# Gated layers: the norm's row factor put onto the gate and up outputs, their inputs split tile by tile, squares added on GpSimd

## What is computed

```
def rmsnorm(x, gain):
    y = xf * lax.rsqrt(jnp.mean(xf * xf, axis=-1, keepdims=True) + EPS)
    return y * gain
def swiglu(h, w_gate_up, w_down):
    gate, up = jnp.split(h @ w_gate_up, 2, axis=-1)
    return (jax.nn.silu(gate) * up) @ w_down
for i in range(DEPTH_2):                       # 2 layers
    h = rmsnorm(x, norm_mix[i])
    x = x + (s5_mixer(h, ...) if i == 0 else dsa_mixer(h, ...))
    x = x + swiglu(rmsnorm(x, norm_ffn[i]), ffn_w_gate_up[i], ffn_w_down[i])
```

## Time and profile before

| what | value |
|---|---|
| time, median of 3 runs | 3164.7 us (3161.42 to 3247.57) |
| the profiled execution | 3160.65 us, span 3158.8 us, clock 0.96 |
| PE busy | 2900.4 us, 92% of the span |
| DVE busy | 1864.0 us, 59% |
| ACT busy | 1393.9 us, 44% |
| POOL busy | 219.7 us, 7% |
| L348 by high_b and weight_parts | 1872 matmuls, 398 ns mean each |
| L716 low part of weights | 185, 1226 ns mean |
| L708 high part of weights | 185, 1060 ns mean |

### The profile page before, as it was taken

The page is one execution under the profiler, slowest core; times in us unless marked ns, Lnnn a source line. Parts: engine busy times, 40 slices in busy tenths (PEclk is TensorE's granted clock), DMA queues, the critical chain, the costliest instruction groups (busy, mean ns, idle before and its releaser), DMA issues.

```text
span 3158.8 us, 35772 instructions
## 1 busy us (share of the span) xinstructions
PE 2900.4 (92%) x12800; PEld 2235.7 (71%) x12800; DVE 1864.0 (59%) x2206; ACT 1393.9 (44%) x1794; POOL 219.7 (7%) x167
## 2 busy tenths in 40 slices
PE   7999999985899999999993678999989999989998
PEld 2548878765677777777772566788867767768887
DVE  3435653564988888888887753333236685343322
ACT  2323233223667777777775323323223435333221
POOL 1100100003930000000001000000001100000000
PEclk9999999996999999999997879999999999999999
DMA  6921722314899989999993802222221110122221
GB/s 236 330 76 60 282 85 94 121 62 161 319 331 352 387 351 387 361 377 369 369 372 108 107 32 75 94 95 106 93 75 67 67 54 1 41 72 101 94 94 67
DMA packets 90801, 546.92 MB, mean 173 GB/s; under 512 B 9232, under 2 KB 18848, under 8 KB 32384
## 3 DMA queue, kind: packets, MB, share of 16 engines
q1 hardware_dynamic: 79584, 485.65, 41.6%
q0 software_dynamic: 10816, 59.58, 5.5%
q10 hardware_dynamic: 288, 0.15, 0.0%
HBM read 516.51 MB, written 41.42 MB: 177 GB/s over the span
## 4 chain that ended last, share of the span: by engine, by line
PE 69%; DVE 17%; issue 6%; DMA 4%; ACT 3%; SPq 1%; POOL 1%; DVEq 0%; ACTq 0%; PEldq 0%; POOLq 0%
PE bank L348 38%; PE bank L286 6%; PE bank L1138 5%; PE bank L1142 4%; PE bank L1141 4%; DVE expert_low L2218 4%; DMA arena<-in_we_stream 2%; ACT expert_high L1587 1%; PE bank L1370 1%; PE bank L1392 1%; PE bank L1383 1%; DMA arena<-in_mod 1%; PE bank L1122 1%; DVE expert_x_low L2303 1%; DVE arena L2320 1%
## 5 line engine op out<-in xcount | busy, mean ns | idle before, releaser
L2218 DVE TENSOR_TENSOR expert_low<-arena,expert_high 128x2048 fp32r<-128x2048 f32 x291 | 684.2, 2382 | 102.7 <-ACT expert_high L1587 85.4
L1587 ACT ACTIVATE expert_high<-arena 128x1024 fp32r<-128x1024 f32 x582 | 597.2, 1057 | 213.4 <-PE bank L1138 117.5
L348 PE MATMUL bank<-high_b,weight_parts 128*128 128x512 f32 x1872 | 592.9, 398 | 29.6 <-DVE low_b L2456 15.9
L716 DVE TENSOR_TENSOR weight_parts<-ring_pages,weight_parts 128x1024 fp32r<-128x1024 f32 x185 | 226.7, 1226 | 557.9 <-ACT weight_parts L708 557.4
L708 ACT ACTIVATE weight_parts<-ring_pages 128x1024 fp32r<-128x1024 f32 x185 | 196.1, 1060 | 591.6 <-PE bank L348 552.4
L348 PEld LDWEIGHTS bank<-high_b,weight_parts 128*128 128x128 f32 x1872 | 352.8, 190 | 121.1 <-issue 36.3
L348 PE MATMUL bank<-low_b,weight_parts 128*128 128x512 f32 x832 | 325.7, 391 | 0.0
L1138 PE MATMUL bank<-expert_high,expert_x_low 128*128 128x512 f32 x768 | 309.5, 403 | 14.1 <-DVE expert_low L2218 10.4
L1141 PE MATMUL bank<-expert_high,expert_x_high 128*128 128x512 f32 x768 | 301.1, 392 | 0.0
L1142 PE MATMUL bank<-expert_low,expert_x_high 128*128 128x512 f32 x768 | 300.6, 391 | 0.0
L348 PE MATMUL bank<-hidden_parts,weight_parts 128*128 128x512 f32 x1056 | 240.0, 389 | 4.3 <-DVE hidden_parts L2502 4.3
(11 more groups left out here) (464 smaller groups left out, 4033.2 us busy)
## 6 DMA issues: line engine op xcount, KB each, us to landing
arena<-in_we_stream SPq DMA_DIRECT2D x294, 1024.0 KB, 6.5
ring_pages<-in_wb_stream SPq DMA_DIRECT2D x93, 1024.0 KB, 4.8
ring_pages<-in_wa_stream SPq DMA_DIRECT2D x49, 1024.0 KB, 4.9
arena<-in_mod POOLq DMA_DIRECT2D x16, 1024.0 KB
xbuf<-arena POOLq DMA_DIRECT2D x25, 512.0 KB, 15.9
arena<-xbuf SPq DMA_DIRECT2D x17, 512.0 KB, 7.3
ybuf<-arena SPq DMA_DIRECT2D x16, 512.0 KB, 2.6
arena<-kd SPq DMA_DIRECT2D x8, 512.0 KB, 24.1
```

What stands on the lines that cost most here:

```text
L348: ins = pe.matmul(o, lhsT, rhs, start=start, stop=stop)
L716: nc.vector.tensor_tensor(low, src, high.bitcast(F32), ALU.subtract).then_inc(weights_split, 1)
L1587: nc.scalar.activation(ehigh[c % HIGH_E][:, at], ring_e[c % RING_E][:, at], ACT.Copy) \
L2218: nc.vector.tensor_tensor(elow[c % RING_E][:], ring_e[c % RING_E], ehigh[c % HIGH_E][:].bitcast(F32), ALU.subtract).then_inc(weights_split ...
```

## The change

The norm of a gated layer commutes with its products: (x * gain * RS) @ W is ((x * gain) @ W) * RS, since RS is one number per token. The change uses that.

- The gated layers' input is now x * gain only. `ffn_tile` (ScalarE) makes its high part straight from `x` with the gain as the scale, and then the tile's square; `ffn_low` (VectorE) makes the low part from `x`, gain and high part in one instruction. Both stand in the loops of the product ahead (`glu`, `wo`), one tile behind the tile of `x` that was just finished.
- `sn2` and `sn4` stand behind the first gate block (`gu00`, `gu10`). Their root and reciprocal are taken after the weight splits of the first pair.
- For each gate block VectorE first writes gate * RS into `st` (an added instruction), ScalarE applies silu in place, VectorE writes up * RS into `product` (was the product with silu) and multiplies by `st` there (added).
- GpSimd adds the eight squares into the first (`squares_summed`, seven additions), and TensorE multiplies only the sum by ones. This holds for `sn3` too. For `sn3` the squares stay behind the last `down` block's splits, and `normed_all` stays.
- `low_g`, `hid_late`, `ffn_in` and the new place of the third squares move buffers, so that inputs of a gated layer can be written while the product ahead still reads its own.

```diff
-JOBS_B += [f"glu{b}" for b in range(2 * KT)] + ["sn2"]
-JOBS_B += [f"gu0{b}" for b in range(2 * FFT)] + [f"down0{j}" for j in range(KT)] + ["sn3"]
+JOBS_B += [f"glu{b}" for b in range(2 * KT)] + ["gu00", "sn2"]
+JOBS_B += [f"gu0{b}" for b in range(1, 2 * FFT)] + [f"down0{j}" for j in range(KT)] + ["sn3"]
...
+            def squares_summed(n):
+                for kt in range(1, KT):
+                    pool.wait_ge(S["b_sq_full"], KT * (n - 2) + kt + 1)
+                    link(nc.gpsimd.tensor_tensor(sqb[n][:, 0, :], sqb[n][:, 0, :], sqb[n][:, kt, :], ALU.add))
+                pool.sem_inc(S["sq_summed"], 1)
+
+            squares_summed(2)
+            squares_summed(3)
             pool.wait_ge(S["b_x_ready"], 2 * KT)
...
             def squares(n):
                 ps = opened(f"sn{n}")
-                for kt in range(KT):
-                    pe.wait_ge(S["b_sq_full"], KT * (n - 2) + kt + 1)
-                    ins = pe.matmul(ps[:], ones[:], sqb[n][:, kt, :], start=(kt == 0), stop=(kt == KT - 1))
-                ins.then_inc(bank_done, 1)
+                pe.wait_ge(S["sq_summed"], n + 1)
+                pe.matmul(ps[:], ones[:], sqb[n][:, 0, :], start=True, stop=True).then_inc(bank_done, 1)
...
+            def ffn_tile(n, kt):
+                act.wait_ge(S["b_x_ready"], KT * 2 * n + kt + 1)
+                nc.scalar.activation(ffn_in[n][0][:, kt, :], x[:, kt, :], ACT.Copy, scale=col("norm_ffn", KT * n + kt)) \
+                    .then_inc(high_ready, 1)
+                squared_tile(2 + 2 * n, kt)
...
             def dense_act(n, n_sig):
-                high_part(high_b, raw, S["b_h_full"], h_count[2 + 2 * n] - KT)
                 for j in range(FFT):
                     weights_high_part(act, ahead(f"down{n}", f"gu{n}", 2 * j), split_to)
-                    ps = result(act, f"gu{n}{2 * j}")
-                    act.wait_ge(S["b_st_used"], n_sig - 1)
+                    if j == 0:
+                        rooted(2 + 2 * n)
                     n_sig += 1
-                    copied(act, nc.scalar.activation(st[:, j % 2, :], ps[:], ACT.Silu), S["b_sig_b"], n_sig,
-                           f"gu{n}{2 * j}")
+                    act.wait_ge(S["b_st_given"], n_sig)
+                    nc.scalar.activation(st[:, j % 2, :], st[:, j % 2, :], ACT.Silu).then_inc(S["b_sig_b"], 1)
...
+            def ffn_low(n, kt):
+                n_high[0] += 1
+                dve.wait_ge(high_ready, n_high[0])
+                high, low = ffn_in[n]
+                nc.vector.scalar_tensor_tensor(out=low[:, kt, :], in0=x[:, kt, :], scalar=col("norm_ffn", KT * n + kt),
+                                               in1=high[:, kt, :].bitcast(F32), op0=ALU.mult, op1=ALU.subtract) \
+                    .then_inc(split_ready, 1)
...
             def dense_dve(n, n_sig, n_x):
-                normed_all(2 + 2 * n, "norm_ffn", KT * n, low_b)
                 for j in range(FFT):
...
+                    gate, up = f"gu{n}{2 * j}", f"gu{n}{2 * j + 1}"
+                    weights_low_part(dve, ahead(f"down{n}", gate[:3], 2 * j), split_to)
+                    if j == 0:
+                        rms(2 + 2 * n)
                     n_sig += 1
+                    copied(dve, nc.vector.tensor_tensor(st[:, j % 2, :], result(dve, gate)[:], RS[:], ALU.mult),
+                           S["b_st_given"], n_sig, gate)
+                    if j < FFT - 1:
+                        weights_low_part(dve, ahead(f"down{n}", gate[:3], 2 * j + 1), split_to)
+                    link(nc.vector.tensor_tensor(product[:, j % 3, :], result(dve, up)[:], RS[:], ALU.mult))
+                    dve.sem_inc(free(up), 1)
                     dve.wait_ge(S["b_sig_b"], n_sig)
...
+                    nc.vector.tensor_tensor(product[:, j % 3, :], product[:, j % 3, :], st[:, j % 2, :], ALU.mult) \
+                        .then_inc(product_ready, 1)
```

74 lines of the change are left out of this document (44 added, 30 removed).

## The result

| what | before | after |
|---|---|---|
| median of the timed runs | 3243.11 us (3161.42 to 3256.53, 20 runs) | 3139.07 us (3132.32 to 3228.15, 20 runs) |
| the profiled execution | 3160.65 us | 3138.67 us |
| ratio of compared runs | | 0.9946, 95% interval 0.9924 to 0.9969 |

Launches of either kernel fall into levels. Over all series of this study, the kernel before has 40 of its 71 launches at 3156 to 3166 us and 31 at 3238 to 3257; the changed kernel has 20 of 33 at 3128 to 3141, 12 at 3157 to 3175 and one at 3228. The ratio leaves out every run more than 1.5% above the lowest of its series: here the highest level alone, in experiments 1, 7 and 9 also one or two runs of the middle one, so the ratios of different series can't be set side by side. The two medians are 104 us apart only because 12 of the 20 launches before are of the highest level.

What follows compares the result with a forecast made beforehand. TensorE's products bound it, broken only where a norm stands between two; 17.7 + 17.7 - 0.4 - 1.7 - 1.8 = 31.5 us off 3160.65 gives 3129.2, plus 1: 3130 us, range 3124 to 3140.

Steps and rivals of the forecast that it cites:

- Start of layer 0: From the end of glu: gu00 follows at once, gu01 starts 17.7 us earlier with contention, 19.5 without.
- Rival (b): GpSimd's additions do not disturb VectorE at layer 0 and sn3 loses only 0.9 us: 3127 us, chance 0.12.
- Start of layer 1: From the end of wo: no contention expected, gu11 starts 17.7 us earlier.
- gu03's weights: Their split stands behind root, reciprocal and silu; just fits, 0.2 us lost per layer, 1.3 if the table load shows.
- Rival (c): The row factor's chain is longer than summed, gu03 comes 1 to 4 us late per layer: 3136 us, chance 0.13.
- Inside the layers: Two more VectorE instructions of 0.69 us per pair of blocks fit into free time and cost nothing.
- rival (e): The longer chain per pair makes each weight split late: slower, 3200 us at 5 us more per pair, chance 0.02.
- rival (d): gu00 or gu10 still waits for the norm, so one layer's start stays as it is: 3148 us, chance 0.04.
- Ends of the layers: Ahead of the down blocks the gap grows from 2.17 to 3.0 us: 0.85 lost, twice, 1.7 us.
- Rival (a): The clock falls behind the new 3.0 us gaps at both gated layers' ends, about 3 us each: 3136 us, chance 0.22.
- sn3: The norm behind layer 0's down blocks waits for seven additions: 1.8 us lost, bounds 0.9 and 1.8, cossin fetch hidden.
- The sum: All terms over the launch: 17.7 + 17.7 - 0.4 - 1.7 - 1.8 = 31.5 us gained, forecast 3130 us.

Runs made afterwards that it cites:

- experiment 1: The changed kernel again, no edit, beside the kernel before: median 3138.34 us against 3165.67, ratio 0.9961.
- experiment 7: Changed kernel with third-norm squares made one by one beside the down blocks and the row factor on the gate alone: median 3148.15 us, ratio 0.9881 to the kernel before.
- experiment 9: The kernel of experiment 7 again, no further edit: median 3154.35 us, ratio 0.9946.
- experiment 3: Changed kernel without the GpSimd additions, TensorE multiplying all eight squares again: 3135.99 us, one execution.
- Experiment 2: Kernel before with only the GpSimd additions of squares, TensorE multiplying the sum: 3259.94 us, one execution.
- experiment 4: Changed kernel with only sn3's squares back on TensorE, without additions there: 3135.17 us, one execution.
- experiment 5: Changed kernel with sn3's squares made one by one beside the down blocks, additions kept: 3213.28 us, one execution.
- experiment 6: Changed kernel with the row factor on the gate's silu alone, one instruction fewer behind the last up block: 3205.98 us, one execution.
- 10 to 12: Thirteen more matmuls in the attention's loop, in the kernel before, the changed one and that of experiment 7: medians 3183.42, 3146.15 and 3138.19 us.

## Why the prediction was right or wrong

**Start of layer 0: right, 1.0 us too little.** gu00 follows `glu` at once and gu01 starts 7.17 us later. I had 8.1. The order of contention was as told, addition 6, low part 6, addition 7, low part 7:

```profile
1965.07 1.29 POOL L920 TENSOR_TENSOR arena<-arena 128x512 f32<-128x512 f32 x1 [8.42 <-ACT arena L1669]
1966.78 1.29 POOL L920 TENSOR_TENSOR arena<-arena 128x512 f32<-128x512 f32 x1 [0.41 <-ACT arena L1669]
```
```profile
1965.44 1.47 DVE L2496 SCALAR_TENSOR_TENSOR low_b<-arena,cols,high_b 128x512 fp32r<-128x512 f32 x1 [0.24 <-DVE arena L2509]
...
1966.84 1.78 DVE L2496 SCALAR_TENSOR_TENSOR low_b<-arena,cols,high_b 128x512 fp32r<-128x512 f32 x1
```

Each low part ends 0.55 us behind its addition (1966.91 behind 1966.36, 1968.62 behind 1968.07), where I had 0.8, and the four overlap a little more than I let them, so TensorE lost 1.3 us and not 1.9. Rival (b), that the additions do not disturb VectorE, falls with experiment 3.

The matmul of the sum was right at 0.88, but only half of it lies ahead of gu01. gu01's first two matmuls are followed by the next after 0.88 us, where in the steady stream it is 0.46:

```profile
1969.94 1.03 PE L348 MATMUL bank<-high_b,weight_parts 128*128 128x512 f32 x2
1970.82 0.40 PE L348 MATMUL bank<-low_b,weight_parts 128*128 128x512 f32 x1
1971.05 0.62 PE L348 MATMUL bank<-high_b,weight_parts 128*128 128x512 f32 x2
1971.51 0.40 PE L348 MATMUL bank<-low_b,weight_parts 128*128 128x512 f32 x1
...
1981.27 0.62 PE L348 MATMUL bank<-high_b,weight_parts 128*128 128x512 f32 x2
```

0.46 ahead of gu01's start and 0.41 inside it make 0.87. So of the 18.65 us gained up to gu01, 0.41 is given back at once.

**Start of layer 1: right**, 18.17 for 17.7, no gap. The excess is again the half of the sum's matmul that comes behind gu11's start (0.41).

**gu03's weights: right that they just fit, and the 0.2 us per layer was not needed.** The chain from the ACT and DVE timelines of the changed kernel:

```profile
1973.21 0.69 ACT L1679 ACTIVATE arena<-bank,eps 128x512 f32<-128x512 f32 x1
1974.00 1.28 ACT L1777 ACT_TABLE_LOAD   x1
...
1978.05 0.63 ACT L1777 ACTIVATE arena<-arena 128x512 f32<-128x512 f32 x1 [2.76 <-DVE arena L2533]
```
```profile
1973.93 3.35 DVE L2382 RECIPROCAL arena<-arena 128x512 f32<-128x512 f32 x1 [0.78 <-ACT arena L1679]
1977.32 0.69 DVE L2533 TENSOR_TENSOR arena<-bank,arena 128x512 f32<-128x512 f32 x1
1979.66 1.23 DVE L721 TENSOR_TENSOR weight_parts<-ring_pages,weight_parts 128x1024 fp32r<-128x1024 f32 x1 [1.65 <-ACT weight_parts L713]
```

The silu's table load runs under the reciprocal, and gu03's low part ends at 1980.89, 10.95 behind gu01's start, where I had 10.7. TensorE comes to gu03 at 1981.27, later than the 10.88 that I had, by the 0.41 above, and does not wait: from gu01's third matmul to the layer's end no two start more than 0.24 us apart. The 0.35 that the layer takes more than before is the second half of the sum's matmul and not this chain; that it looks like the 0.2 summed is chance. Rival (c) falls.

**Inside the layers: right.** No pair is longer, rival (e) falls; gu00 and gu10 do not wait for the norm, and rival (d) falls.

**Ends of the layers: right in the gap, wrong about what decides the clock.** 3.08 us for 3.0. Rival (a) took the gap of 2.17 as safe, from one execution in which both were. Experiment 2 has two gaps of 2.17 with a fall behind each. Counting down blocks over 120.0 us in all profiled executions: 5 of 14 behind gaps of 2.17 and 2.25, 7 of 14 behind gaps of 3.08. These counts are too small to tell the two lengths apart. The place differs more: 9 of 14 gaps of layer 0 have a fall and 3 of 14 of layer 1, and the changed kernel fell in layer 0 three times of three and never in layer 1; no run says why. The same gap of one kernel can go either way (layer 0 in experiments 7 and 9). A fall costs 1.3 to 2.6 us, and mostly 1.6, not 3. The sum had nothing for it and the profile lost 1.63.

**sn3: right**, 1.79 for 1.8, with the matmul at half clock and the fetch hidden, and experiment 4 has it back.

**The sum: right in the stretch it was made for (30.07 for 31.5), wrong as a forecast of the measured difference.** That it came within 1.4 us is luck in part: the terms of the sum together gave 1.0 more than summed and the stages not shown 0.5, against 1.6 lost to a fall of the clock and 1.3 in the attention, both of which the sum had at nothing. The step that failed is the one from the sum to the launch's time: "3160.65 - 31.5 = 3129.2; the median shown stands 4 us above the profiled one, of which I add 1". It takes the rest of the launch as fixed. It isn't: the start of `glu` moves by up to 9 us, and the attention by 24 or by 74 to 84 us, depending on whether a fall of the clock holds on. One of the three times shown before, 3247.57, was by its size of that kind, and I had read it as something apart. Of the changed kernel's runs seven of twenty lie at 3157 to 3174 and stand in the ratio; with them it says 0.5%, without (the lowest level, the lowest runs, the stages) 0.9 to 1.0%.

What is shown: in profiled runs at 3148, 3155, 3206, 3213 and 3260 the half clock in the attention makes the difference (experiments 2, 5 to 7, 9), and with more matmuls there no launch of 17 was in an upper level (10 to 12). No run of the changed kernel at 3157 to 3175 was caught in a profile, but each launch has its span and mean granted clock, and twice the span times the share not granted estimates its time at half clock. That is 264 us on average in the lowest level of the changed kernel, 314 in its three runs at 3157 to 3161 and 355 in the nine at 3167 to 3175; in the kernel before 267 and, in the highest level, 457, which is 190 more, as the 195 of experiment 5's two stretches. So the middle level is half clock too, 50 or 90 us of it; that it lies in the attention is likely and not shown. What stays open is why a fall holds on in one launch and not in another, and why the kernel before was in its highest level in 31 of 71 launches and the changed one in 1 of 33, with the middle level in its place.

## What to carry to other kernels

A factor that commutes with a product can be moved behind it, and the norm's chain then hides under the first block; what it costs shows up at the last block, where each added instruction lies bare, so apply the factor to whichever operand is ready early. Adding squares on GpSimd is worth it where they come one at a time beside other work (5.25 and 6.0 us here) and costs where they come in a bunch (1.8 us), and spreading the squares turns the one case into the other (4.6 us, which is 2.8 better than TensorE's eight products). A change of 1% is to be judged by stages: find the rows that bracket it in several executions, and look how far the rest of the launch moves by itself.

## What the runs showed of the hardware

- The granted clock can stay at half for 48, 65 or 130 us while TensorE is busy throughout (115.35 of 116.00 us), in a stage of small matmuls, where another execution of the same work is back at full speed after 7 us.
- It falls behind some gaps of 2.2 us (5 of 14) and holds behind some of 3.1 (7 of 14).
- Beside GpSimd's additions of 1.29 us, VectorE's instruction with two SBUF inputs goes from 0.73 to 1.59 us each (1.45 to 3.17 for two); beside VectorE's weight splits a GpSimd addition goes from 1.29 to 1.74 us.
- A plain float32 matmul of 128x512 shows as two passes. One in a steady stream of products adds 0.87 us to it, as much as each of eight in a row (7.03 us, 0.88 each), but only 0.46 of that is seen ahead of the next block's start; the other 0.41 stands behind that block's first matmul.
